# The first three passes of a mixture-of-experts block get their token rows by gather from a stored copy, not by products with marks

## The reference

```python
N_EXPERTS = 16; N_GROUPS = 4; TOP_K = 2; D_FF_EXPERT = 256
def _grouped_moe(x, router_w, router_bias, w_gate, w_up, w_down):
    scores = jax.nn.sigmoid((t @ router_w).astype(jnp.float32))
    ...                     # best group of 4 experts, then the best 2 experts in it
    gates = jnp.sum(jax.nn.one_hot(eidx, N_EXPERTS) * wts[..., None], axis=1)
    hid = jax.nn.silu(jnp.einsum('td,edf->tef', t, w_gate)) * jnp.einsum('td,edf->tef', t, w_up)
    y = jnp.einsum('tef,efd->td', hid * gates[..., None], w_down)
```

## Time and profile before

| | |
|---|---|
| median of 3 runs | 1354.31 us (1353.17 to 1354.92) |
| the profiled execution: time, span | 1353.48 us, 1351.7 us |
| PE, DVE, ACT, POOL busy | 96%, 59%, 26%, 23% of the span |
| mean granted TensorE clock | 0.987 |
| layer 0's block: PE from the first L2110 to the last product | 715.5 to about 879 us |
| layer 1's block | 1158.7 to about 1319 us |
| DMA moved over the span | 217.80 MB, mean 161 GB/s |

### The profile page before, as it was taken

One profiled execution on the slowest core, in us unless ns is written; L12 is line 12 of the kernel. 1 busy time (PEld: TensorE's weight loads), 2 busy tenths in 40 slices (PEclk: granted clock), 3 DMA queues, 4 the chain that ended last, 5 costly groups with the idle time before them and its releaser, 6 DMA issues. The chain is left out here.

```text
span 1351.7 us, 22148 instructions
## 1 busy us (share of the span) xinstructions
PE 1300.3 (96%) x7810; PEld 744.8 (55%) x7810; DVE 795.7 (59%) x1757; ACT 350.2 (26%) x781; POOL 305.7 (23%) x536
## 2 busy tenths in 40 slices
PE   8999999999999999999998999999999999899995
PEld 5468675766757667577754433355545454433332
DVE  2777777676776767766666442284353545734327
ACT  3323322222222222222222221113322322132210
POOL 2364434052340523406012000130000000200015
PEclk9999999999999999999998999999999999899998
DMA  7440505225052250532527899840201128389982
GB/s 216 135 112 18 161 8 165 66 74 159 6 165 65 74 159 6 159 128 51 189 94 271 319 407 412 321 152 1 90 30 45 43 75 358 137 336 406 411 321 102
DMA packets 154934, 217.80 MB, mean 161 GB/s; under 512 B 56240, under 2 KB 106800, under 8 KB 154864
## 3 DMA queue, kind: packets, MB, share of 16 engines
q1 hardware_dynamic: 117040, 166.06, 35.4%
q10 hardware_dynamic: 32736, 32.77, 7.4%
q0 software_dynamic: 5088, 18.02, 3.7%
HBM read 183.54 MB, written 33.29 MB: 160 GB/s over the span
## 5 line engine op out<-in xcount | busy, mean ns | idle before, releaser
L541 PE MATMUL bank<-xT,wgu 128*128 128x512 f32 x448 | 196.0, 593 | 0.1
L2143 PE MATMUL bank<-wgu,moe_xgT 128*32 128x512 f32 x1152 | 155.5, 594 | 1.6 <-ACT moe_xgT L2267 1.5
L541 PEld LDWEIGHTS bank<-xT,wgu 128*128 128x128 f32 x448 | 83.8, 191 | 97.0 <-issue 96.8
L1246 DVE SCALAR_TENSOR_TENSOR wgu<-bank,taps,wgu 128x510 f32<-128x510 f32 (+1 forms) x128 | 95.7, 748 | 59.9 <-ACT wgu L843 53.9
L627 PE MATMUL bank<-wd,xT 128*128 128x256 f32 x512 | 119.6, 385 | 0.3 <-DVE res L1341 0.3
L593 PE MATMUL bank<-wd,oT 128*128 128x512 f32 x224 | 105.4, 594 | 0.0
L627 PEld LDWEIGHTS bank<-wd,xT 128*128 128x128 f32 x512 | 95.2, 191 | 16.3 <-issue 3.2
L2143 PEld LDWEIGHTS bank<-wgu,moe_xgT 128*32 128x32 f32 x1152 | 44.9, 110 | 77.4 <-issue 67.7
L2178 PE MATMUL bank<-wd,moe_hidT 128*32 128x512 f32 x704 | 81.5, 604 | 4.3 <-issue 4.3
L2453 DVE TENSOR_TENSOR moe_hid<-moe_silu,bank 128x256 f32<-128x256 f32 x22 | 9.3, 422 | 121.4 <-ACT moe_silu L2273 121.4
L1692 POOL DMA_INDIRECT wgu<-slots_y,fetch x8 | 9.7, 1210 | 260.6 <-issue 246.4
(11 more groups left out here) (376 smaller groups left out, 2328.3 us busy)
## 6 DMA issues: line engine op xcount, KB each, us to landing
wd<-moe_w_down SPq DMA_DIRECT2D x32, 1024.0 KB, 13.7
wgu<-moe_w_gate SPq DMA_DIRECT2D x26, 1024.0 KB, 10.4
wgu<-moe_w_up SPq DMA_DIRECT2D x26, 1024.0 KB, 13.7
wgu<-dn_w_in SPq DMA_DIRECT2D x32, 512.0 KB, 4.5
slots_x<-gains SPq DMA_DIRECT2D x5, 1920.0 KB, 10.4
wgu<-gate_rows SPq DMA_DIRECT2D x14, 512.0 KB, 5.2
wd<-dn_w_out ACTq DMA_DIRECT2D x14, 512.0 KB, 3.9
wd<-dn_w_in ACTq DMA_DIRECT2D x7, 1024.0 KB, 5.4
```

Source lines behind the costliest of these rows:

```text
L541: mm = pe.matmul(bank[:], wqkv[:, ct, k], xT[:, k], start=k == 0, stop=k == KD - 1)
L1246: ins = nc.vector.scalar_tensor_tensor(out=conv[:, ct, lo:hi], in0=bank[:, lo + d:hi + d], scalar=w[:, j:j + 1], in1=conv[:, ct, lo:hi], o ...
L2143: mm = pe.matmul(ps[2][seats].rearrange("p (a f) -> p a f", a=2), xgT[:, j % ROW_BUFS, k, seats], gate_up_of(e)[:, :, k], start=k == 0, st ...
```

## The change

In both blocks SP first stores `res` (the normed tokens, 512 x 1024, 2.1 MB) as it is to a new DRAM tensor `rows_x`. PE multiplies the marks not by `res` but by one column of token numbers (`C_TOK`), which gives for each of the 128 seats of a pass the number of its token. DVE casts that list to `listed` (`keep_list`), and POOL gathers the rows by it from `rows_x` to `x_rows`. This is done for three passes instead of two; the third list needs two more marks. The gathers stand ahead of the scatters on POOL. ACT's copies `keep_rows` are gone. SP loads passes 3 and 4 (before: 2 and 3), ACT 5 to 10; ACT's wait for `scattered` comes a little later. PE runs three more idle products after the lists. The wait for `x_y_ready`, in the branch for crowded experts, is gone. The weights of `fifth` keep their place as SP's requests at the beginning, now behind the stores.

```diff
-PICKED = 2
+PICKED = 3
@@ SP
+            for tt in range(TT):
+                sp.dma_start(t["rows_x"][tt * P:(tt + 1) * P], res[:, tt]).then_inc(t["rows_kept"], 16)
             if layer == 0:
                 load_down(sp, t, dram, layer, 2)
             sp.dma_start(pair_rows(fifth[:, 0]), pick(g_dram, FIXED - 1)).then_inc(gu_in[FIXED - 1], 16)
...
             next_gate_up(5)
             sp.wait_ge(scattered, 16 * 2 * TT)
-            sp.wait_ge(rowsT_full, 2)
-            for j in range(PICKED, PICKED + 2):
+            sp.wait_ge(rowsT_full, 4)
+            for j in range(PICKED, 5):
                 sp.dma_start(x_rows[:, j % ROW_BUFS], rows_of(slots_x, j)).then_inc(rows_loaded[j % ROW_BUFS], 16)
@@ POOL
-            pool.wait_ge(place_ready, 1)
+            pool.wait_ge(t["rows_kept"], 16 * TT * (layer + 1))
+            for j in range(PICKED):
+                pool.wait_ge(place_ready, j + 1)
+                nc.gpsimd.indirect_dma_start(x_rows[:, j], None, t["rows_x"], bass.IndirectOffsetOnAxis(listed[:, j:j + 1], 0),
+                                             bounds_check=SEQ - 1).then_inc(gathered[j], 16)
+            pool.wait_ge(place_ready, PICKED + 1)
             for k in range(2):
                 for tt in range(TT):
                     nc.gpsimd.indirect_dma_start(slots_x, ...
@@ PE
-            def pick_rows(j):
-                pe.wait_ge(hot_ready, 2 * j + 2)
-                for half in range(2):
-                    for tt in range(TT):
-                        mm = pe.matmul(picked_bank(j, half)[:], hots[j][:, tt], res[:, tt, half * 512:(half + 1) * 512], start=tt == 0, stop=tt == TT - 1)
-                    mm.then_inc(picked, 1)
+            def list_rows(j):
+                pe.wait_ge(marks_ready, 1 + 2 * j + 2)
+                for tt in range(TT):
+                    mm = pe.matmul(list_bank(j), hots[j][:, tt], c[:, C_TOK + tt:C_TOK + tt + 1], start=tt == 0, stop=tt == TT - 1)
+                mm.then_inc(ranked, 1)
             for j in range(PICKED):
-                pick_rows(j)
+                list_rows(j)
+            keep_going(3)
             turn_rows(0)
@@ ACT
-            for j in range(PICKED):
-                keep_rows(j)
...
-            act.wait_ge(scattered, 16 * 2 * TT)
-            load_rows(4)
             results(0)
             store(0)
             rowsT(2)
+            act.wait_ge(scattered, 16 * 2 * TT)
             load_rows(5)
@@ DVE
+            def keep_list(j):
+                dve.wait_ge(ranked, j + 2)
+                nc.vector.tensor_copy(listed[:, j:j + 1], list_bank(j)).then_inc(place_ready, 1)
+            keep_list(0)
+            mark_seats(2, 2, 0, 2 * P - 2 * CAP, 3 * CAP - 2 * P)
+            mark_seats(2, 3, 3 * CAP - 2 * P, 0, CAP)
...                       # key, more
+            keep_list(1)
             step(nc.vector.tensor_reduce(place_of[:], more, AX.X, ALU.add))
+            keep_list(2)
```

More of the change, by code:

```diff
@@ L48 @@
 C_TILE = C_SUM + 16
-C_ALL = C_TILE + 16
+C_TOK = C_TILE + 16
+C_ALL = C_TOK + 4
 def constants():
@@ L1945, in mixture @@
         order = sb("order", [1, SORTED], mybir.dt.uint32)
+        listed = sb("listed", [P, PICKED], mybir.dt.uint32)
         owner = sb("owner", [1, EXTRA], mybir.dt.uint32)
@@ L1954, in route_and_run @@
     wgu, wd, x_rows, y_rows, xgT, silu, hid, hidT, upper = (m[n] for n in ("wgu", "wd", "x_rows", "y_rows", "xgT", "silu", "hid", "hidT", "upper"))
-    place, gate2, counts, owner, order, fifth = (m[n] for n in ("place", "gate2", "counts", "owner", "order", "fifth"))
+    place, gate2, counts, owner, order, listed, fifth = (m[n] for n in ("place", "gate2", "counts", "owner", "order", "listed", "fifth"))
     slots_x, slots_y = t["slots_x"], t["slots_y"]
@@ L1986, in route_and_run @@
         returned, fetched = returned_rows(t), t["fetched"][layer]
-        owner, counts_ready = m["owner"], sem("counts_ready")
-        x_block_in, x_rowsT_full, x_rowsT_ready, x_gu_full, x_silu_ready, x_hid_ready, x_hidT_full, x_hidT_ready, x_down_full, x_y_ready = (
-            sem(f"x_{n}") for n in ("block_in", "rowsT_full", "rowsT_ready", "gu_full", "silu_ready", "hid_ready", "hidT_full", "hidT_ready", "down_full", "y_ready"))
+        owner = m["owner"]
+        x_block_in, x_rowsT_full, x_rowsT_ready, x_gu_full, x_silu_ready, x_hid_ready, x_hidT_full, x_hidT_ready, x_down_full = (
+            sem(f"x_{n}") for n in ("block_in", "rowsT_full", "rowsT_ready", "gu_full", "silu_ready", "hid_ready", "hidT_full", "hidT_ready", "down_full"))
         link = sem("link")
-        chosen_ready, ranked, picked, place_ready, scattered = (sem(n) for n in ("chosen_ready", "ranked", "picked", "place_ready", "scattered"))
+        ranked, place_ready, scattered = (sem(n) for n in ("ranked", "place_ready", "scattered"))
+        gathered = [sem(f"gathered{n}") for n in range(PICKED)]
         gu_in, d_in = [sem(f"gu_in{n}") for n in range(FIXED)], [sem(f"d_in{n}") for n in range(RING)]
@@ L2011, in rows_of, with list_bank @@
             return a[j * P:(j + 1) * P]
-        hots = hot, upper
-        def picked_bank(j, half):
-            return ps[4 + 2 * j + half]
+        hots = hot, upper, hot
+        def list_bank(j):
+            return ps[(4, 6, 5)[j]][:, 0:1]
         def result_bank(j, half):
@@ L2123, in turn_rows @@
                 r = j % ROW_BUFS
-                pe.wait_ge(rows_loaded[r], 16 * (j // ROW_BUFS + 1))
+                pe.wait_ge(*((gathered[j], 16) if j < PICKED else (rows_loaded[r], 16 * (j // ROW_BUFS + (r >= PICKED)))))
                 for half in range(2):
@@ L2242, in _ @@
                     pe.wait_ge(x_gatesT_kept, n + 1)
-                    pe.wait_ge(x_y_ready, n + 1)
                     for part in range(2 * TT):
@@ L2252, in _ @@
         def _(act):
[L2253 to L2256, removed]
             def load_rows(j):
@@ L2434, in _ @@
             nc.vector.tensor_copy(owner[:], owner_f[0:1])
-            nc.vector.tensor_copy(counts[:], ends[0:1, NE - 1:NE]).then_inc(counts_ready, 1)
+            nc.vector.tensor_copy(counts[:], ends[0:1, NE - 1:NE]).then_inc(place_ready, 1)
             many = crowded(dve)
@@ L2530, in _ @@
                     for half in range(2):
-                        ins = nc.vector.tensor_copy(spare_y[0:CAP, half * 512:(half + 1) * 512], ps[4 + half][0:CAP])
-                    ins.then_inc(x_y_ready, 1)
+                        nc.vector.tensor_copy(spare_y[0:CAP, half * 512:(half + 1) * 512], ps[4 + half][0:CAP])
                     dve.wait_ge(x_gatesT_full, n + 1)
@@ L3100, in program @@
             "gain_cols": ctx.enter_context(nc.sbuf_tensor("gain_cols", [P, 2, 2, KD], F32)),
+            "rows_kept": ctx.enter_context(nc.semaphore("rows_kept")),
             "gain_cols_in": ctx.enter_context(nc.semaphore("gain_cols_in")),
             "beta_rows": nc.dram_tensor("beta_rows", (2 * NV, SEQ), F32, kind="Internal").ap(),
+            "rows_x": nc.dram_tensor("rows_x", (SEQ, D), F32, kind="Internal").ap(),
             "A_rows": nc.dram_tensor("A_rows", (P // 2, BLK * BLK), F32, kind="Internal").ap(),
```

27 lines of the change are left out of this document (16 added, 11 removed).

## The result

| | median us (runs) | ratio to before, 95% interval |
|---|---|---|
| before | 1356.29 (15; 1351.49 to 1359.90) | 1 |
| changed | 1360.75 (15; 1356.67 to 1367.40) | 1.0035 (1.0023 to 1.0047) |
| changed, timed again beside the last experiments | 1361.21 (12) | 1.0033 (1.0017 to 1.0049) |

The change costs 4.5 us, where 7.3 us of gain were forecast. The profiled execution of the changed kernel took 1360.70 us (span 1358.8), that of before 1353.48, near the fast end of what before's 15 runs took. The traces are therefore compared by block, from the block's first product (L2110, now L2121).

What follows compares the result with a forecast made beforehand. Each block is bound by PE, then by bytes until `down(6)`. Bytes decide: 4.0 and 2.5 us sooner make 6.5, plus 0.8 of net corrections is 7.3 us, from 1354.31 to 1347.0; range 1342.0 to 1352.0.

Steps and rivals of the forecast that it cites:

- rival (a): Before `down(6)`: bytes are no bound, so PE's side counts in full, 10.2 or 13.6 us; middle 1342.4; chance 0.19.
- PE's side: At each block's beginning: PE gains 7.0 and 6.6 us, less 1.7 each for the clock: 5.3 and 4.9.
- lost each time: On PE after a gap of some 2 us: 32 products take 5.34 us for 3.62, so 1.7 us lost.
- the one on `scattered`: On DVE: `residual(0)` waits for the scatters, but PE has enough to do before `rowsT(2)`; no wait, 0.
- DVE's chain: On DVE up to `place`: list waits, marks and casts delay the scatters by 2.3 us, bounds 1.4 and 3.5.
- The sharing: DMA engines, scatters beside gate/up 5: both need 15.6 us at 405 GB/s, done at about 751.
- the slower side: Whole kernel: the outcome of running slower than before by more than about 0.2% (2.7 us); chance 0.07.
- The bytes: DMA up to `down(6)`: expert 10's weights land 4.0 and 2.5 us sooner, net +0.4 a block after corrections.
- H: Theory of the follow-up runs: late scatters hold DVE, and DVE by way of ACT holds PE before gate/up 2.
- (b): DMA queue gives all back: SP's wait and late scatters leave 0.5 to 1 us; 1353; chance 0.13.
- (c): POOL is held up, writing the gathers' descriptors only after DVE's chain; 1364.8; chance 0.08 together with a late gather.
- (d): A right gather lands after 739.3, 13 us from issue, with the same effect on PE; chance 0.08 with POOL held up.

Runs made afterwards that it cites:

- Residual late: The changed kernel with `residual(0)` moved behind `results(0)` and `rowsT(2)` on DVE; ratio to before 0.9974, 1352.93 us.
- down weights 5 ahead: The changed kernel with `residual(0)` behind `rowsT(2)`, and SP asking for down weights 5 ahead of gate/up 8; ratio to before 0.9985.
- third list late: The changed kernel with `residual(0)` behind `rowsT(2)`, list 2's marks and cast behind `place`, its gather behind the scatters; ratio to before 1.0002.
- Lists by ACT: The changed kernel with `residual(0)` behind `rowsT(2)`, and the three lists cast by ACT in place of DVE; ratio to before 0.9951, 1350.23 us.
- gate/up 5 behind the scatters: The changed kernel with SP asking for gate/up 5 after its wait for the scatters and two row loads; ratio to before 1.0002.

## Why the prediction was wrong

**What bounds the kernel.** Right: PE at the beginning, then bytes to `down(6)`. Residual late and down weights 5 ahead show it, and rival (a) falls: with residual late PE's leads of 5.2 and 4.9 us at gate/up 2 were 1.0 and -0.9 at `down(6)`, and the waits moved with the requests.

**PE's side.** Forecast 7.0 and 6.6 us sooner at turn 0, less the clock 5.3 and 4.9; measured 5.6 and 5.2 at the transposes. Right in sum, by two errors that cancel. A list takes 1.6 to 1.8 us, not 1.0 (24 records in 5.28 and 4.72): the forecast's own upper bound, eight records at half the clock, came true, since the granted clock was 0.50, its lower level, during the lists of layer 0 and for most of them in layer 1. In a layer where it was 1.00 (third list late, layer 1) 16 such records took 1.95 us, the 1.0 a list that was forecast. The stretch of the lists in the changed kernel, and that of those 16 records in third list late; the clock is the last but two:

```profile
724.60:729.80 5.20, 5.20 (x25) 5.14 (x25) 2.21 (x10) 0.00 (x0) 1.70 (x2) 0.50 1.02 395
```

```profile
1168.40:1170.50 2.10, 1.95 (x16) 1.86 (x16) 1.21 (x6) 0.00 (x0) 0.00 (x0) 1.00 1.02 417
```

Against that, PE did not stand idle as I thought, so the clock's 1.7 us did not come on top: the three idle products took until turn 0 (4.64 and 4.26 us for 6 records, mostly at the lower clock). In layer 0 the rows of pass 0 had landed 0.3 us before turn 0, in layer 1 1.7 us before: there the idle products, not the gather, held PE. By block the first gather was issued 0.9 us later than forecast in layer 0 and 0.1 in layer 1. The 1.7 us "lost each time" was also a misreading of the earlier trace rows: layer 1's gap of 2.16 us cost no clock.

**The step that failed** is the one on `scattered`: "PE has gate/up 1, `down(0)` (a `down` is 3.62 us) and turn 2 to do before it wants them, so I put no wait here". PE then waited 4.6 and 5.0 us, and the clock after it cost 1.7 and 1.3. I had seen DVE's queue (`residual(0)`, `results(0)`, `rowsT(2)`) and dismissed it, with the landing at about 751, and I had not seen that ACT's `store(0)` and `rowsT(2)` hang on it too. What stands between the landing and PE takes 4.3 us. With the landing forecast, 35.5 us into layer 0's block, PE would have been free to go on at 39.8, just as it wanted to (its turn 2 and hidden 1 were done at 40.0): there was no room, and no wait only if nothing was late. DVE saw the landing 40.3 us into the block, 4.8 later, and PE waited 4.6. In layer 1 the same sum gives 34.8 forecast and 39.8 measured, and a wait of 5.0.

Two sizes made the landing late. *DVE's chain*: 2.3 us, bounds 1.4 to 3.5; measured 4.05 and 3.5, of which 3.2 and 2.6 are the waits for the three lists: the list's error on PE came three times over on DVE. *The sharing*: I let scatters and weights run at the full 405 GB/s; in layer 0 they had 273 in the first five microseconds, most of it the weights'. The chain's error makes the scatters start 1.8 and 1.2 us later than forecast, which leaves 3.0 and 3.8 us to the sharing. By my own words, what there may be of it was in the low end; it was no rival of its own, and with it the slower side had 0.07.

**The bytes.** Forecast: expert 10's weights 4.4 and 2.9 us sooner. With residual late, which takes H away, `down(6)`, which waits for them, began 1.0 us sooner in layer 0 and 0.9 later in layer 1. The 1.8 and 1.1 us that the scatters started later than I had them, and the 2.2 us of idle engines (0.8 taken, bounds 0 and 2), would account for 3.2 of the 3.4 missing in layer 0 and 2.5 of the 3.8 in layer 1; no run takes these terms apart. Lists by ACT, which start the scatters 1.3 and 1.0 us later than before, where 2.3 was forecast, gave 0.9951, that is 6.6 us: with both delays out, a gain of the forecast's size is there. It is no proof of the forecast's sum, since the scatters start sooner than the forecast had them.

**Rivals.** (b) named SP's wait and late scatters as eating the gain, which they did in part; (c) and (d) did not happen: the gathers took 1.00 to 1.21 us each on POOL beside DVE's chain, and the first landed 6.3 us from issue in layer 0 and 4.6 in layer 1, where 6.0 and 5.0 were taken. The delay that the Trainium skill warns of ("SBUF — State Buffer", the "DVE blocks DMA" trap) did not show; its rule is for DVE operations in a two-port mode, and no run here shows whether any of this chain's small operations was in one. The slower side came from a third place.

## What to carry to other kernels

Where a change delays a transfer, list every instruction that waits for its landing *and what is queued behind that instruction*, on other engines too where they wait for the queued work, and price the landing with the transfers that it will then meet: here 4.1 and 3.5 us of delay became 9 to 10 us at the landing, since the transfer slid into the next one. A wait for a short product stands in the waiting engine's queue each time; give it to the engine that is idle (ACT here), not to the one on whose chain the next step hangs. Where bytes bound a later stage, moving requests only moved the wait here.

## What the runs showed of the hardware

A product of one column cost PE as much as the short ones that count ranks: 0.12 us a record at the full granted clock (16 in 1.95 us), where those took 0.125 with 16 to 64 columns. At the lower level of the clock, 0.50, it was 0.22 (24 in 5.28 us). In the changed kernel's layer 0 the clock was 0.50 through the lists and stayed there until 733 us; in the kernel before, where PE picks with 512 columns at this place, it was also 0.50 from 724 to 726 us, but 1.00 from 727 on.

A scatter from POOL beside weight requests of SP got little of the engines at first (0.18 MB of 1.21 between 744.5 and 749 us): the last scatter of layer 0 took about 11 us from issue to landing with sharing and 5.0 without (gate/up 5 behind the scatters).

The clock's cost after a gap of 2 to 3 us before `down(6)` is not certain: 5.34 us for 32 records in some blocks, 3.6 in others, with the same gap.
